# First tiles and sample rows of a hybrid decoder step, reordered

## The reference, cut to what matters

```python
u = rmsnorm(x, norm_g)
lx, lg, sb, scg, sh, sg, q, qg, mg = jnp.split(u @ w_in, SPLIT_POINTS, axis=-1)
xc, new_lru_buf = causal_dwconv(lx, lru_buf, lru_conv_w)           # A: conv(4), gated recurrence
hs, new_h = rglru(xc + lru_conv_b, lru_h, ...)
z_a = (hs * silu(lg)) @ lru_wo
cy, new_sc_buf = causal_dwconv(scg * sh, sc_buf, sconv_w)          # B: conv(3)
z_b = (silu(sg) * sb * cy) @ sconv_wo
p = softmax(einsum('bthd,bmhd->bhtm', qh, mem_k) / sqrt(128))      # C: 4 heads, 256 memory rows
o = einsum('bhtm,bmhd->bthd', p, mem_v)
z_c = (o * silu(qg)) @ xa_wo
g_a, g_b, g_c = split(sigmoid(mg), 3)
y = (g_a * z_a + g_b * z_b + g_c * z_c) @ w_out
out = rmsnorm(x + y, final_norm_g)
```

## Time and profile before

| | |
|---|---|
| median of 3 runs (lowest to highest) | 769.9 us (769.24 to 771.2) |
| the profiled execution | 770.45 us |
| span of its slowest core, core 5 | 768.8 us |
| spans of the 8 cores | 760.0 to 768.8 us |
| mean granted TensorE clock of core 5 | 0.986 of 2.4 GHz |
| TensorE busy, of the span | 728.3 us (95%) |
| VectorE, ScalarE, POOL busy | 57%, 44%, 16% |

### The profile page before, as it was taken

The page is one execution under the profiler, slowest core; times in us unless marked ns, Lnnn a source line. Parts: engine busy times, 40 slices in busy tenths (PEclk is TensorE's granted clock), DMA queues, the critical chain, the costliest instruction groups (busy, mean ns, idle before and its releaser), DMA issues.

```text
span 768.8 us, 11026 instructions; the slowest of 8 cores (760.0 to 768.8 us)
## 1 busy us (share of the span) xinstructions
PE 728.3 (95%) x4128; PEld 340.4 (44%) x4128; DVE 438.7 (57%) x456; ACT 339.7 (44%) x429; POOL 126.3 (16%) x116
## 2 busy tenths in 40 slices
PE   1889999999999999999999989999999899999995
PEld 1444544444444444444444434444445344444442
DVE  3446333795977959779598375555423131324776
ACT  4454456767767776676851411111211112112343
POOL 1000000001110011100103312232444332222000
PEclk9999999999999999999999999999999899999998
DMA  8984170313113131120424048444666546366434
GB/s 185 270 227 76 29 145 6 52 27 55 29 15 45 25 55 29 18 38 1 69 34 90 1 78 157 130 92 132 119 98 87 92 62 117 55 185 230 192 117 160
DMA packets 26419, 69.67 MB, mean 91 GB/s; under 512 B 2192, under 2 KB 6416, under 8 KB 26240
## 3 DMA queue, kind: packets, MB, share of 16 engines
q0 software_dynamic: 11472, 31.90, 27.9%
q1 hardware_dynamic: 14896, 37.08, 14.5%
HBM read 91.15 MB, written 9.82 MB: 131 GB/s over the span
## 4 chain that ended last, share of the span: by engine, by line
PE 85%; DVE 5%; DMA 5%; issue 2%; ACT 2%; DVEq 0%; POOL 0%; ACTq 0%; POOLq 0%; SPq 0%
PE PP L372 79%; PE PQ L372 4%; DMA R<-cv 2%; DMA R<-ck 2%; PE PQ L467 1%; DMA pT<-prm 1%; DVE R L783 1%; PE PQ L1033 1%; DVE R L1036 0%; DVE R L1134 0%; DVE R L995 0%; DVE R L1130 0%; DVE R L790 0%; DVE R L984 0%; ACT gA L453 0%
## 5 line engine op out<-in xcount | busy, mean ns | idle before, releaser
L372 PE MATMUL PP<-uT,R 128*128 128x512 bf16 (+1 forms) x2272 | 496.0, 374 | 2.1 <-DVE uT L475 1.5
L372 PEld LDWEIGHTS PP<-uT,R 128*128 128x128 bf16 x2272 | 214.1, 98 | 257.0 <-issue 15.5
L1125 ACT ACTIVATE R<-PP 128x1024 f32<-128x1024 f32 x48 | 49.2, 1024 | 213.5 <-PE PP L372 211.7
L1134 DVE SCALAR_TENSOR_TENSOR R<-R,PP 128x1024 f32<-128x1024 f32 x32 | 39.1, 1221 | 111.1 <-PE PP L372 101.4
L372 PE MATMUL PP<-R 128*128 128x512 bf16 (+1 forms) x360 | 84.5, 385 | 0.0
L1138 POOL TENSOR_TENSOR R<-R 128x1024 f32<-128x1024 f32 x16 | 37.6, 2349 | 127.7 <-DVE R L1134 111.4
L372 PEld LDWEIGHTS PP<-R 128*128 128x128 bf16 (+1 forms) x360 | 34.7, 98 | 42.6 <-issue 3.2
L696 DVE SCALAR_TENSOR_TENSOR R<-R,pT 128x1024 f32<-128x1024 f32 x36 | 45.7, 1283 | 2.5
L1141 POOL TENSOR_TENSOR R<-R 128x1024 bf16<-128x1024 f32 x16 | 37.6, 2350 | 57.4 <-DVE R L1134 44.6
L1130 DVE SCALAR_TENSOR_TENSOR R<-R,PP 128x1024 f32<-128x1024 f32 x16 | 19.5, 1220 | 45.5 <-PE PP L372 27.2
L372 PE MATMUL PP<-gB,R 128*128 128x512 bf16 x192 | 44.1, 379 | 0.0
(11 more groups left out here) (171 smaller groups left out, 688.8 us busy)
## 6 DMA issues: line engine op xcount, KB each, us to landing
R<-wl POOLq DMA_DIRECT2D x32, 512.0 KB, 8.9
R<-xp SPq DMA_DIRECT2D x16, 512.0 KB, 9.6
R<-ck SPq DMA_DIRECT2D x16, 512.0 KB, 5.1
y_p<-R SPq DMA_DIRECT2D x15, 512.0 KB, 2.6
R<-wl POOLq DMA_DIRECT2D x8, 768.0 KB, 11.3
uT<-xp SPq DMA_DIRECT2D x9, 512.0 KB, 9.1
R<-cv POOLq DMA_DIRECT2D x16, 256.0 KB, 6.7
R<-wkv POOLq DMA_DIRECT2D x1, 2048.0 KB, 14.3
```

Of the source, the lines that this page charges most:

```text
L372: S.op("pe", lambda e, l=l, r=r, i=i: e.matmul(out_ap, l, r, start=(i == 0), stop=(i == n - 1)), reads=reads, writes=[wtok], inc=(last_inc ...
L1125: S.op("act", lambda e, pp=pp, th_=th_: e.activation(out=th_, in_=pp[:], func=AF.Tanh, scale=0.5), reads=[tk], writes=[tth])
L1134: S.op("dve", lambda e, th_=th_, zp=zp: e.scalar_tensor_tensor(out=th_, in0=th_, scalar=1.0, in1=zp, op0=ALU.add, op1=ALU.mult), reads=[tt ...
```

## The change

- The parameters prm go through ScalarE's queue, ahead of its first operation, and not through POOL's; they are padded from 82 to 128 columns.
- The first weight tile is issued when x tile 0 has landed (was: 1), the second when tile 2 has (was: 3). x tile 8 is issued right behind x tile 7, without waiting for the third weight tile.
- For the first three tiles, the square sum of tile ti + 2 and the scaling of tile ti + 1 are recorded ahead of the transposes and the copy of tile ti. All scaling is on VectorE.
- Unit q0 of groups 0 and 1 is made in two halves of 256 rows each: of group 0 behind tiles 1 and 3, of group 1 behind tiles 7 and 8.
- gen_ab yields twice more at its end, and the softmax once more, so that the keys come two merge steps later and the values three.
- The sample rows' attention product (sample_out) is recorded behind row tile 3 of the last stage.

```diff
-        S.dma("pool", "prm", pT[:], prm[:, :], writes=[t_pT])
+        S.dma("act", "prm", pT[:], prm[:, :], writes=[t_pT])
         for ti in range(4):
             x_load(ti)
-        w_issue_upto(0, after=[t_x[1]])
-        w_issue_upto(1, after=[t_x[3]])
+        w_issue_upto(0, after=[t_x[0]])
+        w_issue_upto(1, after=[t_x[2]])
         x_load(4, [tslot[0]])
         x_load(5)
         w_issue_upto(2, after=[tslot[0]])
         x_load(6, [tslot[1]])
         x_load(7)
+        x_load(8)
         w_issue_upto(3, after=[tslot[1]])
-        x_load(8, [tslot[2]])
...
-        def start_unit(name, g):
+        def start_unit(name, g, part=None):
             views, wtk = w_get(name)
             pp, tk = next_pp()
+            c0, c1 = g * 512, (g + 1) * 512
+            if part is not None:
+                c0 += part * 128
+                c1 = c0 + 256
...
+            if ti < 3:
+                n_sq(ti + 2)
+                n_scale(ti + 1)
             n_tr(ti)
-            if ti + 1 < NT:
+            if 3 <= ti < NT - 1:
                 n_scale(ti + 1)
+            if ti in (1, 3):
+                start_unit("q0", 0, ti - 1)
             if ti == 3:
-                pending += [(nm, 0) for nm in SU]
-            if pending:
+                pending += [(nm, 0) for nm in SU[1:]]
+            if pending and ti > 3:
                 start_unit(*pending.pop(0))
-            if ti + 2 < NT:
+            if 3 <= ti < NT - 2:
                 n_sq(ti + 2)
-            if ti in (7, 11, 15):
+            if ti == 7:
+                start_unit("q0", 1, 0)
+                pending += [("q0", 1, 2)] + [(nm, 1) for nm in SU[1:]]
+            if ti in (11, 15):
                 pending += [(nm, ti // 4) for nm in SU]
...
             S.dma("sp", "out", o_so[:, :], SO_t[:], reads=[t_SO])
+            yield
+            yield
...
             S.op("dve", lambda e: e.tensor_copy(PT, PX[:, 0:128].rearrange("p (c x) -> p c x", c=2)), reads=[tPX], writes=[t_PT])
             yield
+            yield
...
         for ti in range(NF - 1):
             f_mm(ti)
             f_sq(ti)
             if ti:
                 f_out(ti - 1)
+            if ti == 3:
+                sample_out()
```

More of the change, by code:

```diff
@@ L234, in build_program @@
     wab_d = din("wab", [128, 2 * NCH * 128])
-    prm = din("prm", [128, 82])
+    prm = din("prm", [128, 128])
     sit_d = din("sit", [128, NCH * 8 * TS])
@@ L263, in build_program @@
         onesb = sb("onesb", [128, 128], BF16)
-        pT = sb("pT", [128, 82], F32)
+        pT = sb("pT", [128, 128], F32)
         dv = sb("dv", [128, 24], F32)
@@ L451, in n_scale @@
                  reads=[t_st0[ti]], writes=[t_st0[ti]])
[L452 to L456, removed]
             S.op("dve", lambda e, xb_=xb_, xn_=xn_, nr=nr, ti=ti: e.tensor_scalar(out=xn_[0:nr, :], in0=xb_[0:nr, :],
@@ L522, in build_program @@
         wab = wab_t.rearrange("p (a n d) -> p a n d", a=2, n=NCH)
-        def start_unit(name, g):
+        def start_unit(name, g, part=None):
             views, wtk = w_get(name)
             pp, tk = next_pp()
+            c0, c1 = g * 512, (g + 1) * 512
+            if part is not None:
+                c0 += part * 128
+                c1 = c0 + 256
             for b in range(2):
[L528 to L531, removed]
+                pairs = [(views[b][k], uT[:, k, c0:c1]) for k in range(KC)]
+                mm_group(pp[:, b * 512:b * 512 + c1 - c0], pairs, [wtk] + u_toks(c0, c1), tk, last_inc=(b == 1))
+            src = pp[:].rearrange("p (a t) -> p a t", a=2)[:, :, 0:c1 - c0]
             if name == "q0":
@@ L1192, in build_program @@
             pass
[L1193 to L1203, removed]
         xr, t_xr = [], []
@@ L1290, in f_out, with sample_out @@
             S.dma("sp", f"yo{ti % 4}", dst, yr_[0:nr, :], reads=[tyr])
+        def sample_out():
+            for i_ in range(2):
+                vxo, txo = w_get(f"xo{i_}")
+                for jj in range(4):
+                    j = 4 * i_ + jj
+                    mm_group(PS[:, j * TS:(j + 1) * TS], [(vxo[jj][k], og[:, k, T:TT]) for k in range(4)],
+                             [txo] + [t_og[c][4] for c in range(4)], tPS, last_inc=(j == 7))
+            S.op("dve", lambda e: e.scalar_tensor_tensor(out=ths[:, :, 0:TS], in0=ths[:, :, 2 * TS:3 * TS], scalar=1.0,
+                                                         in1=PS[:, 0:8 * TS].rearrange("p (j b) -> p j b", j=8), op0=ALU.add,
+                                                         op1=ALU.mult), reads=[tPS, t_ths], writes=[t_ths])
+            S.op("dve", lambda e: e.tensor_tensor(out=mT[:, :, T:TT], in0=ths[:, :, 0:TS], in1=accs, op=ALU.add),
+                 reads=[t_ths, t_accs], writes=[t_mT[j][2] for j in range(8)])
         for ti in range(NXR):
@@ L1335 @@
     shared = {
-        "wl": f(np.concatenate(parts)), "wkv": f(wkv), "wab": f(wab), "prm": f(prm.T), "w_out": f(w_out[0]), "final_norm_g": f(final_norm_g),
+        "wl": f(np.concatenate(parts)), "wkv": f(wkv), "wab": f(wab), "prm": f(np.pad(prm.T, ((0, 0), (0, 46)))), "w_out": f(w_out[0]), "final_norm_g": f(final_norm_g),
     }
```

## The result

| | before | after |
|---|---|---|
| median | 769.9 us | 762.0 us |
| runs | 769.24 to 771.2 | 759.31, 761.38, 762.62, (824.53) |
| ratio | | 0.9884, 95% interval 0.9852 to 0.9915 |
| profiled execution | 770.45 us | 762.62 us |
| span of its slowest core | 768.8 us (core 5) | 761.1 us (core 0) |

The account below looks back on a forecast made before the run. TensorE was taken as the bound, so time could be won only where it waits or runs at 1.2 GHz after waiting. 770.45 - 4.9 - 3.9 - 2.6 = 759.05, said as 759.0 us, range 753.5 to 766.0.

Parts of the forecast that it names:

- Start, forecast 4.9 us: First projection units: earlier loads, scaling ahead of copies and half units bring TensorE forward; 4.9 us, from -0.7 to 6.6.
- the first unit's start is set by weights: Start: a sign that the forecast is wrong, which took tile 2 to set the first unit's start, at 15.2.
- two falls of the clock: Start: if the clock falls in both pauses (2.0 and 1.9 us), each costs about 1.7 us, leaving 3.2 of 6.6.
- if pauses of 2 us drop the clock: Start: a sign that the forecast is wrong, which expected a clock of 1.00 from 35 to 50.
- The three units behind keep their distance: Start, after the first unit: the next three follow as before, so the fourth ends at 24.0 + 11.8 = 35.8.
- I expect them by 24 and 29: Start: weights 2 and 3, sharing with seven tiles, land by 24 and 29 and are wanted at 28 and 32.
- The first rival: Start bound by DMA: tile 2 late beside weights, clock drops; start gains -0.7 to 1, total 764 us; chance 0.13.
- Keys, forecast 3.9 us: First key product, two merge steps later: the 2.74 us wait and 1.7 of low clock go; net 3.9, from 0.7 to 4.4.
- half a loss: Keys: three key loads, not two, now meet a weight pair; 0.5 us taken off for late landing.
- The second rival: Key loads behind weights replace the stall: three at 5.5 us each, 16.5 lost, 775 us, slower; chance 0.03.
- Values, forecast 0: Value loads behind the weights, wanted two steps later: only their number changes, the 3.8 us of waits stay; 0.
- Attention product, forecast 2.6 us: Before the last stage: the 0.85 us wait goes and 1.7 us of low clock too; 2.6, or 0.85 if that stays.

Follow-up runs that it names:

- t_xfirst: The changed kernel with six value buffers, plus x4 issued behind x3, x5 and x6 behind the first weights, x7 behind the second, x8 behind the third: 753.22 us.
- s_xfirst: The changed kernel with its four value buffers, plus x4 issued behind x3, x5 and x6 behind the first weights, x7 behind the second, x8 behind the third: 759.59 us.
- t_prm: The changed kernel with six value buffers, plus the parameters loaded on POOL's queue again, as before: 757.73 us.
- t_wold: The changed kernel with six value buffers, plus the first two weight tiles issued behind x tiles 1 and 3 again, as before: 757.2 us.

## Why the prediction was right, and where it was off

*Start, forecast 4.9 us.* Core 5, for which it was worked out, reached the merge stage 4.9 us earlier. The second half unit ended at 25.1 (forecast 24.0, or 25.7 at 1.2 GHz), and the next group's unit came at 44.76 (43.2): right in mechanism there. The split cost next to nothing: a half took 3.57 us at 1.2 GHz and 1.91 at 2.4, for 3.45 and 1.73 in the sum. But the first half unit's time is luck in part.

The first half unit came at 15.06 (15.2) by another release than forecast. Rows of core 5: tile 2's square sum, the copy of tile 1, and the first weights, issue to landing.

```profile
9.85 1.04 ACT L439 ACTIVATE gA<-R 128x1024 bf16<-128x1024 f32 x1
...
13.04 1.22 DVE L470 TENSOR_TENSOR uT<-PQ,pT 128x1024 bf16<-128x1024 bf16 x1
...
R<-wl POOLq DMA_DIRECT2D x1, 512.0 KB, 9.0
```

Tile 2 was there by 9.85 (forecast 11.0), and the copy of tile 1 ended at 14.26 (15.0). The first weights, for which I had "in at 5.2 + 6.1 = 11.3, more with sharing", took 9.0 us from 5.84 on, to 14.8. Before they were asked for 2.8 us later, took 6.1 us and landed at the same 14.8. So the sign "the first unit's start is set by weights" did come, on five of the eight cores; on core 5 it cost 0.8 us, and the tiles' being early hid it.

Of the two falls of the clock I had taken off half, and one of the two came. In the first pause (2.16 us) it fell, so that the second half took 3.25 us and not 1.91; the second (1.62 and 0.66 us) left it at 1.00. With one fall the sum gives 6.6 - 1.7 = 4.9, as measured. Cores differ: the first pause dropped the clock on cores 0, 2, 5 and 7, and not on the other four: the sign "if pauses of 2 us drop the clock" came on half of them. The window holds the second half on core 5 (clock 0.79):

```profile
20.00:28.00 8.00, 6.17 (x35) 4.12 (x36) 3.90 (x6) 3.48 (x7) 0.00 (x0) 0.79 1.03 204
```

On six of the eight cores the start was off: they gained -0.2 to 4.5 us, the two without a wait for tiles 4 to 6 4.9 and 6.6. The step that failed is "The three units behind keep their distance". Tiles 4 to 6 stand between these units, and for that stretch the sum asks only when weights 2 and 3 land ("I expect them by 24 and 29"). On core 0 the two were issued at 16.16 and 19.21 (the issue to landing of each):

```profile
R<-wl POOLq DMA_DIRECT2D x1, 512.0 KB, 11.7
```

```profile
R<-wl POOLq DMA_DIRECT2D x1, 512.0 KB, 13.7
```

That is 27.9 and 32.9, later than forecast and still in time for their units; before, they took 11.0 and 12.5 us on this core. But tile 6, which is issued behind the second weights, at 18.7, came only at 33.1:

```profile
R<-xp SPq DMA_DIRECT2D x1, 512.0 KB, 14.4
```

Over all cores tiles 5 and 6 land 1.2 and 0.5 us earlier than before (the table of the loads above), and the units behind tiles 4 and 6 want to run 2.6 and 2.3 us earlier (core 5: 25.68 for 28.30, 33.87 for 36.17). So on core 0 ScalarE waited 1.96 us for tile 6, and a fall of the clock followed. t_xfirst shows the cause: with these tiles asked for earlier no core of its trace waits, and the gain is 5.8 us (4.8 in s_xfirst, where some waits stay). The first rival, that the start is bound by DMA, was thus right in part: core 0's -0.2 lies in its range, but I gave the delay to tile 2, and it was tiles 4 to 6.

*Keys, forecast 3.9 us.* 3.7 in the mean. On core 5 4.8 (6.0 less 1.2 of moved work): its late key load of the earlier trace rows, for which I had taken off half a loss, went as well. The second rival didn't show.

*Values, forecast 0.* Right for the mean of after (4.9 us of waits and low clock before, 4.3 after), but the term decides which core is slowest: core 0 lost 4.5 us of waits and 3.4 of low clock, core 5 0.8 and nothing. Before, core 5 had lost 3.8 and some 3.4 there: 6.4 us gained on the core of the sum, by a term that stood at nothing. The third pause, costed at nothing, cost 1.5 us beside the kernel before.

*Attention product, forecast 2.6 us.* The wait went on every core; the fall of the clock had stood on only four of eight, and so 1.7 in the mean. The 2.6 was right for core 5 and the other three.

*The slowest core.* This is where the 2 to 3 us between forecast and result are. I summed the terms on the core that was slowest before, and took it to stay near the slowest. For that core the sum missed by 6.8 us: 11.4 forecast, 18.2 measured, most of the difference in the values. The mean span fell by 9.6 to 9.9 us, the time by 7.9, since other cores gained less: in the profiled run the slowest is the one whose x tiles and values both come late, and which core is slowest changes from run to run (0, 1 and 3 in the three of after). That the time came so near the forecast is thus partly luck: what core 5 gained beyond it doesn't count, and what core 0 lacked does.

## What to carry to other kernels

When work is moved forward, ask of every load that it needs when that load is issued and what the issue waits for: tiles that were in time before came late here, and asking for them earlier gave about 1.7 us at the same DMA share. What is won on the slowest core is not what the program wins when waits for transfers differ from core to core and from run to run; look at the spans of all cores, and sum on the mean beside the slowest. Waits that a sum counts as nothing "as before" can be the best place to go on: two more buffers gave 5 us, more than any part of the change.

## What the runs showed of the hardware

- An earlier issue didn't bring the first weights earlier, with x tiles 0 to 3 in flight beside them: issued at 5.12 they took 10.2 us and released the first half unit at 15.53 (t_prm, core 0), issued at 8.32 they took 6.9 us and released it at 15.42 (t_wold, core 3). In the mean of the 8 cores they land at 15.1 to 15.7 us in all 14 kernels, issued at 5.8 to 8.9.
- The parameters, 64 KB on ScalarE's queue, took 5.8 us to land on core 0, and tile 0's square sum started at 6.75 there; with the parameters on POOL's queue (t_prm) it started at 4.66 on the same core (tile 0, issue to landing, mean of 8 cores: 5.2 us in after, 4.2 in before and in t_prm):

```profile
4.66 1.06 ACT L439 ACTIVATE gA<-R 128x1024 bf16<-128x1024 f32 x1 [0.67 <-DMA R<-xp]
```

- A wait of TensorE for data doesn't always cost the clock: in after, value waits of 3.1 to 4.5 us in sum were followed by 1.2 GHz on cores 0, 3, 4 and 6 (3.4 us lost on each), and 3.4 us of them on core 2 weren't.
- A converting load held the DMA engines longer for its bytes than a plain one. From 21 to 29 us of before (core 5), the weights on POOL's queue (the first line) and the x tiles on SP's moved about as many packets and MB, in 71% and 32% of the engines' time. That this is why the order of the loads counts was not tested.

```profile
q0 software_dynamic: 233, 0.89, 71.1%
q1 hardware_dynamic: 216, 0.77, 32.2%
```
